# Strassen units for the gates of the first branch in a hybrid mLSTM / sparse-attention / memory-attention block

## The reference

```
h = rms_norm(x, norm_g)
proj = h @ w_in                      # its last 3 * 1024 columns are the gates
y_a, y_b, y_m = mLSTM(...), sparse attention(...), memory attention(...)
g = sigmoid(gate).reshape(B, S, 3, 1024)
merged = g[0] * (y_a @ w_branch[0]) + g[1] * (y_b @ w_branch[1]) + g[2] * (y_m @ w_branch[2])
x = x + merged @ w_out
```

## Time and profile before

| | us |
|---|---|
| median of three runs | 962.19 (961.67 to 962.60) |
| the profiled execution | 962.06 |
| its span in the profile | 960.0 |
| TensorE busy | 954.0 |
| VectorE busy | 707.4 |
| ScalarE busy | 535.2 |
| GpSimd busy | 346.1 |

### The profile page before, as it was taken

The page is one execution under the profiler, slowest core; times in us unless marked ns, Lnnn a source line. Parts: engine busy times, 40 slices in busy tenths (PEclk is TensorE's granted clock), DMA queues, the critical chain, the costliest instruction groups (busy, mean ns, idle before and its releaser), DMA issues.

```text
span 960.0 us, 13409 instructions
## 1 busy us (share of the span) xinstructions
PE 954.0 (99%) x4897; PEld 839.3 (87%) x4897; DVE 707.4 (74%) x1079; ACT 535.2 (56%) x810; POOL 346.1 (36%) x247
## 2 busy tenths in 40 slices
PE   9999999999999999999999999999999999999998
PEld 7888888888989988988988888898998989988887
DVE  6878987688996676686687565895766958634586
ACT  6877644465456456546573422585765857732251
POOL 0200834456327137136120081362714527107500
PEclk9999999999999999999999999999999999999999
DMA  8624222144531531531354335616043150738312
GB/s 283 245 88 132 89 88 73 58 132 132 166 97 56 176 111 43 155 112 64 121 207 153 122 110 163 221 34 197 1 138 93 33 154 1 258 92 312 125 45 87
DMA packets 105156, 119.27 MB, mean 124 GB/s; under 512 B 4772, under 2 KB 80136, under 8 KB 104332
## 3 DMA queue, kind: packets, MB, share of 16 engines
q1 hardware_dynamic: 105084, 118.53, 38.1%
q10 hardware_dynamic: 16, 0.00, 0.0%
HBM read 106.45 MB, written 12.07 MB: 123 GB/s over the span
## 4 chain that ended last, share of the span: by engine, by line
PE 95%; DVE 3%; DMA 1%; ACT 1%; issue 1%; SPq 0%; DVEq 0%; ACTq 0%
PE proj L781 42%; PE proj L1141 12%; PE proj L1290 9%; PE att L1311 7%; PE proj L1311 5%; PE att L1361 3%; PE proj L951 2%; PE att L1105 2%; PE att L1123 2%; PE att L1070 1%; PE proj L1247 1%; PE att L1113 1%; PE att L1048 1%; PE att L1094 1%; DVE score L2397 1%; PE att L1247 1%
## 5 line engine op out<-in xcount | busy, mean ns | idle before, releaser
L781 PE MATMUL proj<-hT_hi,w_hi 128*128 128x512 f32 x328 | 129.0, 393 | 0.0
L781 PE MATMUL proj<-hT_hi,w_lo 128*128 128x512 f32 x328 | 128.0, 390 | 0.0
L781 PE MATMUL proj<-hT_lo,w_hi 128*128 128x512 f32 x328 | 127.8, 390 | 0.0
L2132 DVE TENSOR_TENSOR w_lo<-w_raw,w_hi 128x2048 fp32r<-128x2048 f32 x28 | 68.5, 2447 | 52.9 <-ACT w_hi L1411 48.9
L1411 ACT ACTIVATE w_hi<-w_raw 128x2048 fp32r<-128x2048 f32 x28 | 53.6, 1914 | 73.2 <-PE proj L781 71.7
L781 PE MATMUL proj<-y_hi,w_hi 128*128 128x512 f32 x192 | 75.2, 392 | 0.7 <-ACT arena L1750 0.7
L781 PE MATMUL proj<-y_hi,w_lo 128*128 128x512 f32 x192 | 74.8, 390 | 0.0
L781 PE MATMUL proj<-y_lo,w_hi 128*128 128x512 f32 x192 | 74.7, 389 | 0.0
L781 PEld LDWEIGHTS proj<-hT_hi,w_lo 128*128 128x128 f32 x328 | 61.6, 188 | 13.1
L781 PEld LDWEIGHTS proj<-hT_lo,w_hi 128*128 128x128 f32 x328 | 61.6, 188 | 12.3
L781 PEld LDWEIGHTS proj<-hT_hi,w_hi 128*128 128x128 f32 x328 | 61.6, 188 | 12.2
(11 more groups left out here) (522 smaller groups left out, 2924.0 us busy)
## 6 DMA issues: line engine op xcount, KB each, us to landing
w_raw<-w_in_in SPq DMA_DIRECT2D x36, 512.0 KB, 4.5
w_raw<-w_in_in SPq DMA_DIRECT2D x56, 256.0 KB, 3.7
w_raw<-w_branch_in SPq DMA_DIRECT2D x10, 1024.0 KB, 7.6
merged<-w_in_in SPq DMA_DIRECT2D x38, 256.0 KB, 3.7
merged<-w_in_in SPq DMA_DIRECT2D x14, 512.0 KB, 5.9
w_raw<-w_in_in SPq DMA_DIRECT2D x6, 1024.0 KB, 5.3
w_raw<-w_mem_kv_in SPq DMA_DIRECT2D x10, 512.0 KB, 6.8
yF<-x_in SPq DMA_DIRECT2D x8, 512.0 KB, 7.5
```

The costliest lines, as they stand in the source:

```text
L781: ins = mm(ps, lhs[a](k, k0), rhs[b](k, k0), start=(first and k == 0 and j == 0), stop=(last and k == KH - 1 and j == 2))
L2132: V.tensor_tensor(w_lo[:, kh, :, 0:n], w_raw[:, kh, :, 0:n], w_hi[:, kh, :, 0:n].bitcast(F32), ALU.subtract).then_inc(w_lo_done, 1)
```

## The change

The gates of the first branch are computed in two units of seven Strassen products, each with 512 of the 1024 gate columns. A product has two halves of 128 gate columns and 256 tokens, over half of the depth. Unit 0 makes the gates of output columns 512 to 1023 in tabs (g_of[0]), unit 1 those of columns 0 to 511 in g_second. The token sums are those of the heads' units (s_parts), so the tiles of y_hi and y_lo are split only when the product that reads the same memory is done. The weights come in blocks of 256 columns: unit 0's into w_raw, unit 1's into merged, which is therefore reloaded after the last low part. GpSimd makes four weight sums for each unit. The operands rotate through six slots. ScalarE saves products 0, 2, 3, 7, 8 and 9 from PSUM to SBUF, VectorE adds 1, 4, 5, 10, 11 and 12, and 6 and 13 go from PSUM through the sigmoid. Then the branch product runs as two whole panels (GA is now two panels), each followed by four merges. The sums and loads of the output projection follow in the queues.

The diff, cut to what decides the order of the work:

```diff
-GA = _plan.take(4, 6, (4,) * 4)
+GA = _plan.take(2, 2, (2,) * 4)
+GATE_UNITS, GATE_SLOT = 2, (4, 0, 1, 2, 3, 4, 0, 1, 2, 3, 4, 5, 2, 3)
+GATE_RAW, GATE_SUM = "acaadbcaaadbcc", {2: 1, 3: 3, 5: 2, 6: 4, 8: 5, 9: 7, 11: 6, 13: 8}
...
 # SyncE
+            gate_raw(0, "a")
+            gate_raw(0, "b")
+            sp.wait_ge(op_low, A_OPLOW + last + 10)
+            gate_raw(0, "c")
+            gate_raw(0, "d")
...
             sp.wait_ge(a_half, 2 * A_HEADS - 1)
+            for slot in "abdc":
+                gate_raw(1, slot)
+            sp.wait_ge(op_low, G_OP + PRODUCTS)
+            load(GA[0], [(wb[0], 0, 512)])
+            load(GA[0] + 1, [(wb[0], 512, 512)])
+            sp.wait_ge(op_low, G_OP + 2 * PRODUCTS)
             sp.dma_start(merged[:, :], merged_kept).then_inc(kept_back, 16)
-            load(GA[0] + 1, [(wb[0], 0, 512)])
-            load(GA[0] + 2, [(wi, 512 + C_GATE, 256), (wb[0], 512, 256)])
             sp.wait_ge(a_y, 2 * A_HEADS)
+            sp.wait_ge(u_done, G_DONE + 2 * 12)
             for slot, dst, kh, c in (("d", out_b22, 1, 1), ("b", out_b12, 0, 1), ("a", out_b11, 0, 0), ("c", out_b21, 1, 0)):
...
-            load(GA[0] + 3, [(wi, 768 + C_GATE, 256), (wb[0], 768, 256)])
...
 # TensorE
-            gates_of(GA, {2: [lambda: a_numerators(g)], 5: [lambda: a_turn_h(g)]})
-            branch_of(GA, y_split(3))
-            with pe.Fori(2, 4) as j:
-                gated(GA, j)
+            def gate_product(n, rhs, to, start, before):
+                w = [op[GATE_SLOT[n]].rearrange("p (k n) -> p k n", k=KH) for op in (g_op_hi, g_op_lo)]
+                pe.wait_ge(op_low, G_OP + n + 1)
+                for f in range(2):
+                    pe.wait_ge(*before(f))
+                    for k in range(KH):
+                        for j, (a, b) in enumerate(((0, 0), (0, 1), (1, 0))):
+                            ins = mm(to[f][:, 0:HALF_T], w[a][:, k, f * P:(f + 1) * P], rhs[b](k), ...)
+                    ins.then_inc(u_done, 1)
+            gate_product(0, h_half(0, 0), first_pair, True, lambda f: (a_atd, 4 * A_HEADS))
+            gate_product(1, h_half(KH, 0), second_pair, True, lambda f: (u_added, G_ADDED))
+            a_numerators(g)
+            gate_product(2, h_half_sum(1), second_pair, True, lambda f: (u_added, G_ADDED + f + 1))
+            gate_product(3, h_half_sum(2), first_pair, False, lambda f: (u_saved, G_SAVED + f + 1))
+            gate_product(4, h_half_sum(3), second_pair, False, lambda f: (u_saved, G_SAVED + f + 3))
+            a_turn_h(g)
+            gate_product(5, h_half_sum(0), first_pair, False, lambda f: (u_saved, G_SAVED + f + 5))
+            gate_product(6, h_half(KH, HALF_T), first_pair, False, lambda f: (u_added, G_ADDED + f + 5))
+            gate_product(7, h_half(0, 0), last_pair, True, lambda f: (a_hnd, 4 * A_HEADS))
+            gate_product(8, h_half_sum(1), second_pair, True, lambda f: (u_added, G_ADDED + f + 3))
+            gate_product(9, h_half_sum(2), last_pair, False, lambda f: (u_saved, G_SAVED + f + 7))
+            gate_product(10, h_half_sum(3), second_pair, False, lambda f: (u_saved, G_SAVED + f + 9))
+            gate_product(11, h_half_sum(0), last_pair, False, lambda f: (u_saved, G_SAVED + f + 11))
+            gate_product(12, h_half(KH, 0), first_pair, True, lambda f: (u_read, G_READ + 4))
+            gate_product(13, h_half(KH, HALF_T), last_pair, False, lambda f: (u_added, G_ADDED + f + 9))
+            pe.wait_ge(u_added, G_ADDED + 12)
+            last_branch_panel(0, [(ys_lo, 3 * KT), None])
+            last_branch_panel(1, None)
...
 # ScalarE, after the last head
+            gate_save(0, low, g_block(0, 0, 0))
+            gate_high(2)
+            gate_high(3)
+            a_norm(g)
+            gate_high(4)
+            gate_save(2, mid, g_block(0, 1, 1))
+            gate_high(5)
+            gate_save(3, low, g_block(0, 1, 0))
+            gate_sigmoid(g_block(0, 0, 0), 2)
+            gate_high(6)
+            gate_high(7)
+            a_finish(g)
+            gate_high(8)
...
+            gate_sigmoid(g_block(1, 0, 0), 12)
+            gate_last_sigmoid(13, top, g_block(1, 0, 1))
             act.wait_ge(w_landed[1], (GA[1] + 1) * 16)
             A_(w_hi[:, 1], w_raw[:, 1], ACT.Copy).then_inc(w_hi_done, 1)
             split_hi(GA[0] + 1, 0, GA[1] + 2, 512)
...
             act.wait_ge(t_done, A_TDONE + OUT_SUMS + 2)
             out_high(1)
+            split_hi(GA[0] + 1, 1, GA[1] + 2, 512, (3, GA[2][3] + 1))
+            split_hi(OUT[0], 0, OUT[1] + 1, 512)
...
 # VectorE, after the last head
+            gate_low(1)
+            gate_low(2)
+            a_denominators(g)
+            gate_add(1, mid, g_block(0, 0, 0), 2)
+            gate_low(3)
+            a_variance(g)
+            gate_low(4)
+            a_gated(g)
+            gate_low(5)
+            gate_low(6)
+            gate_low(7)
+            gate_add(4, mid, g_block(0, 1, 0), 6)
+            gate_low(8)
+            gate_add(5, low, g_block(0, 1, 1), 4)
+            gate_low(9)
+            gate_low(10)
+            gate_low(11)
+            split_lo(GA[0], 0, 512)
+            gate_low(12)
+            y_low(range(2, 4), 0)
+            y_low(range(4, 6), 2)
+            gate_low(13)
+            gate_add(10, mid, g_block(1, 1, 0), 12)
+            y_low(range(6, KT), 4)
+            gate_add(11, top, g_block(1, 1, 1), 10)
+            y_low(range(0, 2), 6)
+            gate_add(12, low, g_block(1, 0, 0), 8)
             split_lo(GA[0], 1, 512)
             split_lo(GA[0] + 1, 0, 512)
...
+            for b in range(4):
+                gated_merge(0, b)
...
+            dve.wait_ge(g_merged, 12)
             out_low_part(1)
+            split_lo(GA[0] + 1, 1, 512)
+            split_lo(OUT[0], 0, 512)
+            early_lows()
+            for b in range(4):
+                gated_merge(1, b)
...
 # GpSimd
+            gate_first_sums(0)
+            gate_next_sum(0)
             a_gate(A_HEADS - 1, 1)
             a_powers(A_HEADS - 1)
+            gate_last_sum(0)
+            gate_first_sums(1)
+            gate_next_sum(1)
+            gate_last_sum(1)
```

More of the change, by code:

```diff
@@ L1204, in _ @@
                     f_panel(i, 0, (P, 0), {3: [lambda: b_turn_qk(r)]})
[L1207 to L1216, removed]
-                panel(j + sec[0], [(b, j + sec[2][b], w_as_lhs(b * P), all_tokens(hT if b < 2 else yT), S, None)
-                                   for b in (2, 3, 0, 1)])
             def branch_panel(q, before, hooks=None):
@@ L1346, in y_block, with last_branch_panel @@
+            gate_product(13, h_half(KH, HALF_T), last_pair, False, lambda f: (u_added, G_ADDED + f + 9))
+            def last_branch_panel(q, before):
+                panel(GA[0] + q, [(b, GA[2][b] + q, w_as_lhs(b * P), all_tokens(yT), S, before if b == 0 else None)
+                                  for b in range(4)])
+            pe.wait_ge(u_added, G_ADDED + 12)
+            last_branch_panel(0, [(ys_lo, 3 * KT), None])
+            last_branch_panel(1, None)
             def y_block(k0, t0):
@@ L1821, in _ @@
                 b_body(i)
-            def first_gates(sec):
-                for b in range(4):
-                    act.wait_ge(proj_done[b], sec[2][b] + 1)
-                    A_(g_sig[b], banks[b][:, :], ACT.Sigmoid).then_inc(bank_empty[b], 1)
-            def gates(sec, j, n, blocks=(0, 1)):
-                for b in blocks:
-                    act.wait_ge(proj_done[b], j + (sec[2][b] + 1))
-                    act.wait_ge(g_merged, n * 2 + (b - 1))
-                    A_(g_sig[b], banks[b][:, :], ACT.Sigmoid).then_inc(bank_empty[b], 1)
             def ym_high(k):
@@ L2094, in _ @@
             out_sums_high(0)
-            gates(GA, 3, 7, (0,))
+            act.wait_ge(proj_done[3], OUT[2][3])
+            act.wait_ge(g_merged, 14)
             merged_high(4)
             merged_high(5)
-            gates(GA, 3, 7, (1,))
             act.wait_ge(g_merged, 16)
@@ L3116, in _, with gate_sum, gate_first_sums, gate_next_sum @@
                 a_gate(h, 0)
+            def gate_sum(u, out, left, right):
+                for half in range(2):
+                    at = slice(half * 512, (half + 1) * 512)
+                    ins = G.tensor_tensor(g_raw[u][out][:, at], g_raw[u][left][:, at], g_raw[u][right][:, at], ALU.subtract)
+                ins.then_inc(t_done, 1)
+            def gate_first_sums(u):
+                pool.wait_ge(*g_landed_of(u, "b"))
+                pool.wait_ge(op_low, G_OP + PRODUCTS * u + 1)
+                gate_sum(u, "a", "b", "a")
+                pool.wait_ge(*g_landed_of(u, "d"))
+                gate_sum(u, "b", "d", "b")
+            def gate_next_sum(u):
+                pool.wait_ge(op_low, G_OP + PRODUCTS * u + 3 - u)
+                gate_sum(u, "a", "d", "a")
+            def gate_last_sum(u):
+                pool.wait_ge(t_done, G_SUM + 4 * u + 3)
+                pool.wait_ge(op_low, G_OP + (2, 13)[u])
```

(7 more changed lines are left out.)

183 lines of the change are left out of this document (115 added, 68 removed).

## The result

The changed kernel takes 984.26 us (981.91 to 985.51, five runs) against 962.19 for the kernel before on the same chip (961.67 to 962.64, five runs): 1.023 times as long, 95% interval 1.0219 to 1.0241. The forecast was 975.0 and its range ended at 982. The sign was right. Of the 22 us, 13 were forecast.

A forecast was written before the change was run, and what follows sets the result against it. PE, busy for 99% of the span, was taken as the bound. From 962.06 us, -3.2 + 1.9 + 3.3 + 1.0 + 7.0 + 3.0 = +13.0 gave 975 us, with an 8 in 10 range of 963 to 982.

The forecast's parts named there:

- The saving (-3.2): Gate products on PE: 336 matmuls of 256 columns take 40.3 us instead of 43.5, saving 3.2 us.
- Wait A: Before product 2: PE waits for DVE's addition of product 1, queued behind the denominators; 1.9 us, between 1.6 and 2.1.
- B: Before product 6: PE waits for DVE's addition of product 5, queued behind low part 8; 3.3 us, between 1.6 and 3.7.
- Wait C: Before product 13: sum 8 waits for low 12, and DVE work stands ahead of the needed addition; 1.0 us taken.
- Wait D: Second half of second branch panel: its weights queue behind output weights awaiting POOL's late sums; 7.0 us, 5.4 to 9.9.
- Wait E: Second output product: the additions that free its banks stand on DVE behind a low part and merges; 3.0 us, 0 to 5.2.
- Operands 0 and 1 are ready: Start of the gate products at 827: PE begins product 0 with both operands ready, so no wait was counted.
- I stay with the rows: DVE beside POOL: low parts priced 1.2 to 1.6 us from trace rows, not as waiting a whole POOL piece, 1.29 more.
- the fourth rival: PE's clock drops after the waits before product 6 and in the second branch panel: 978 to 981 us, chance 0.13.
- The first (only the gate stage stalls): Output weights are loaded and summed in time, so the tail's two waits vanish: 965 us, between 963 and 968, chance 0.21.
- The second and third: Gate stage rivals: product 6's wait covered, 960.7 us, chance 0.12; no difference, 961 to 964 us, chance 0.06.

The follow-up runs named there:

- the three of the gate stage: Changed kernel with POOL's first weight sums held back and, on DVE, the additions of products 1 and 5 put first: 979.79 us.
- all six edits: Changed kernel plus POOL's sums later, additions 1 and 5 first, output loads early, second panel's half ahead of output weights, merges ahead of half-tile sum: 966.30 us.

## Why the prediction was right in sign and short in size

**The saving (-3.2): right.** The pitch is 0.120, as taken from the earlier trace rows, and two units of seven products are 40.3 us of PE work. No run ever kept it.

**Wait A, 1.9, and B, 3.3: right in place and size.** They measured 1.71 and 3.18, released by DVE's additions as predicted, and each went when its addition was put first. For B the size came out and the times did not: PE was ready at 855.6 instead of 850.7 and went on at 858.8, where the chain was to end between 852.3 and 854.4. The delay at product 1 had moved both. What the steps did not say is that they sit on one chain: PE's delay at A was a credit at B, so A taken alone is worth 0.3 and not 1.7.

**Wait C, 1.0: half right.** It measured 0.38, since PE came to it late. Without B ahead of it the same order costs 2.34. The price 1.7 with which I bounded it was below that.

**Wait D, 7.0: right.** Product 13 ended at 884.0 by the chain (880.89 + 3.12), which is X. SP issued merged 5 us later as counted, and POOL's sums began at 904.23, X + 20.2 where the count gave X + 21.3. It measured 6.44, and the mechanism was shown by moving the loads.

**Wait E, 3.0: right.** It measured 3.80, and fell to 0.3 when the merges went first.

A to E sum to 15.5 where 16.2 was forecast; that it is so near is in part luck, since C came out 0.6 smaller and E 0.8 larger. The 9 us by which the forecast fell short come from two steps.

**First failed step: "Operands 0 and 1 are ready", and "I stay with the rows".** The step looked at the high part of product 0 only. The low part of product 1 stands on DVE behind four short subtractions of the turned head, and I moved POOL's sums beside them. I had priced such company by the one long subtraction in the earlier trace rows, 3.33 for 2.29, and allowed a short one 0.4 more at the most (1.2 to 1.6). But the 1.04 lost there is what one subtraction loses whatever its width: the four short ones, 128 to 512 columns wide, lost 1.06 to 1.09 each and took 6.06 instead of 1.69. The rule of the Trainium skill that I weighed and put aside, one blocked piece for each subtraction, gives 4 x 1.29 = 5.2 more as an estimate, where 4.4 was measured. I had applied it to the waits below only. This step cost 2.5 us of waiting and 1.5 at half clock.

**Second failed step: the clock stood outside the sum.** It was the fourth rival with 0.13, on the ground that pauses of the old run had never moved it. Those pauses were short (the longest wait of PE in the old run is 1.5 us, the next 0.7), so they said nothing about waits of 3 and 7 us. In the run four waits were followed by the lower level, the shortest of 2.48 us, and it cost 7.8 us. The Trainium skill (TensorE: Matmul & The Clock Gate, "Why this matters for your kernels") warns that idle gaps between bursts of matmuls send PE back to the lower level. This trace agrees behind four of its six waits. The rival's estimate, a block of 12 matmuls lost at half rate after each wait, 2.7 us, was close for E (2.8) and too high for the others (1.5, 1.5, 1.9). In the sum at B, D and E, the three waits of 3 us and more that I had forecast, it would have added 6.2 (as measured) to 8.1 (3 x 2.7): 981 to 983.

**The rivals.** The first (only the gate stage stalls) is what the run with the loads early comes near to, 969.69 us where it gave 965; the wait before product 1 and the half clock in the stage are the difference. The second and third fell on B, which is a chain from POOL's power as its steps said. The fourth happened in kind, behind B and D and behind two waits that it did not name, and its 978 to 981 was still too low.

## What to carry to other kernels

When a bound engine is given waits that it did not have, price its clock behind each of them, and not as a side case: here 18 us of waits brought 7.8 more. An early load queued behind one whose buffer is not free is a late load, so put loads in a queue in the order in which their buffers come free. Edits that shorten waits on one chain don't add up (A alone gave nothing, three together 4.5 of 10), while edits on separate chains nearly did (the loads alone 14.6 and the three of the gate stage 4.5 are 19.1, and all six edits gave 18.0). The merges put first were worth 5.9 alone and nothing once the loads were early, since both remove wait E. So follow each wait to where it would turn up next before counting a gain.

## What the runs showed of the chip that I had not expected

The clock's fall does not wait for a long pause. It came in the changed kernel behind 2.48 us, in the version with POOL's sums reordered behind 2.14, with the three edits of the gate stage behind 2.32, and did not come behind 1.71, 1.69 or 1.66, nor in one run behind 2.34. At the lower level matmuls of 256 columns start 0.213 us apart instead of 0.120, which is 1.78 times and not twice as long:

```profile
835.20 0.41 PE L1376 MATMUL proj<-hT_hi,w_lo 128*128 128x256 f32 x1
835.41 0.41 PE L1376 MATMUL proj<-hT_hi,w_hi 128*128 128x256 f32 x1
```

Where DVE and POOL meet, the one that starts second pays. In the changed kernel POOL's piece at 825.48 was under way when the subtraction at 825.86 came, and the subtraction lost 1.09 us. POOL's next pieces then took 1.74, 1.60 and 1.44 beside the other three. In the run with POOL's sums held back DVE began first, at 826.52, and took its usual 1.22, while POOL's piece took 2.21:

```profile
826.69 2.21 POOL L3247 TENSOR_TENSOR w_raw<-w_raw 128x512 f32<-128x512 f32 x1 [4.34 <-DVE a_atl L2959]
828.87 1.29 POOL L3247 TENSOR_TENSOR w_raw<-w_raw 128x512 f32<-128x512 f32 x1
```

The 9.47 us of its six pieces are four of about 1.29 and two, 2.21 and 2.27, that met a subtraction of 1024 columns; the mean of 1.58 hides this. Transfers made no such difference: pieces without a subtraction beside them took 1.27 at a DMA share of 1.05 (at 855.95 in the changed kernel) and 1.26 at 0.00 (at 860.67).
